# Expert selection placed one head earlier among the gathers, and up rows taken from the first free group on, in a two-layer transformer kernel on one core

## The chip, the cores and the metric

The kernel runs on one core of one Trainium2 chip. The metric is the device time of one execution in microseconds (us), lower is better. The engines named below are PE (TensorE, matrix products), DVE (VectorE), ACT (ScalarE), POOL (GpSimd, here the issuer of the gathers), and SP (SyncE, issuer of plain loads). All loads and gathers share the core's 16 DMA engines.

## The reference, cut to what matters

Two layers over 256 tokens of width 2048. The first is attention plus a state-space branch, followed by a retrieval block of single-neuron experts; the second has dilated attention and latent attention. The change lies in the retrieval block:

```
q = (ht @ w_query).reshape(t_, PEER_HEADS, 2, PEER_HALF)          # 8 heads, 2 halves
v1, i1 = lax.top_k(s1, 16); v2, i2 = lax.top_k(s2, 16)            # scores against 128 keys each
cand = (v1[..., :, None] + v2[..., None, :])                      # 256 candidates
top_s, pos = lax.top_k(cand, 16); idx = take_along_axis(...)      # 16 experts of 16384
gate = jax.nn.softmax(top_s, axis=-1)
u_sel = expert_down[idx]; act = einsum('tkd,td->tk', u_sel, hb)   # 128 down rows per token
w = gate * gelu(act)
return einsum('tk,tkd->td', w, expert_up[idx])                    # 128 up rows per token
```

## The kernel before, in words

The 256 tokens are two tiles of 128, and 8 retrieval heads for each tile make 16 "heads" here, 0 to 15. The order is 0 and 1 (tile 0), 2 and 3 (tile 1), and so on, so that four heads share one round of keys. Each head has 16 experts per token. **Row k.n** is the n-th down row of head k for all 128 tokens: one gather of 128 x 2048 floats, 1.05 MB. **Dot k.n** is the DVE instruction that multiplies row k.n with the tokens and sums (L2229).

**POOL** issues the gathers in order of k.n (`load_down`, L2219), each by the expert numbers of its head. There are 8 places for down rows (`DOWN_BUFS`), so row k.n may be issued only when the dot 8 rows earlier has ended. Before row 0 of heads 2, 4, 8 and 12, POOL also waits for `experts_ready`, the expert numbers that DVE selects. Among the gathers stand "early" up rows (`load_up`, L2270, 128 x 1280 floats, 0.66 MB, the left five eighths of an up row): one after each of rows 3.5 to 3.15, 7.5 to 7.15, 11.6 to 11.15, and one after each row of heads 14 and 15. This order isn't changed.

**DVE** runs a loop over heads h = 0 to 14 and slots n = 0 to 15; slot (h, n) holds dot (h+1).n, then what `rows_dve` puts there, then for h = 13 and 14 the marking of a group (below). `rows_dve` spreads the selection (`choose`) of later heads over such slots in seven steps: step 0 and 1 take the best 16 of 128 key scores, steps 2 and 3 the best 16 of 256 sums, steps 4 and 5 turn positions into expert numbers (step 5 releases `experts_ready`, L2142), step 6 finishes the gates. Selection number 2 is for heads 2 and 3, number 3 for heads 4 to 7, number 4 for heads 8 to 11, number 5 for heads 12 to 15. ACT takes the exponentials for the gates between steps 3 and 6 (`take_gates`).

**The dense part.** The right three eighths of the up rows aren't gathered. For these the weights are spread into a matrix over all 16384 experts, per tile in 32 groups of 4 tokens (64 groups in all): DVE marks (`mark_group`, 1 + 4 instructions, L2366 and L2371), PE multiplies (`spread_group`, L2381), ACT stores (`take_group`, L2389). Groups 0 to 28 stand in the slots of h = 13 and 14, groups 29 to 63 in a free loop behind the last head. From group 32 on, the second tile's, the weights of that tile must have been turned by PE (`turn_weights(pe, 1)`) and stored by ACT (`take_weights(act, 1)`). Then `dense_rows` (L2411) multiplies with the up rows' right part, which SP loads.

**Up rows in the middle.** Up rows 64 to 95 are handled in 16 pairs in the free loop: of each pair PE sums the first (`sum_up`, L2313), with a diagonal matrix from ACT (`spread_weight`), and DVE adds the second (`add_up`, L2279). They have 5 places. All later up rows, 96 to 255, are added by DVE alone, while the dense products run on PE. `add_sums` (L2323) adds a PSUM sum to the result; `add_sums(dve, 1)` must come before PE begins the next sum.

## Time and profile before

| | us |
|---|---|
| median of 3 runs (3607.11 to 3608.49) | 3607.83 |
| the profiled execution, its own time | 3608.36 |
| its span, first to last instruction | 3606.6 |

| stretch of the span | us | what runs |
|---|---|---|
| 870.85 to 1420.55 | 549.70 | dots of heads 1 to 11 |
| 1420.55 to 1644.20 | 223.65 | dots of heads 12 to 15, groups 0 to 28 |
| 1644.20 to 1740.20 | 96.00 | groups 29 to 63, up rows 64 to 95 |
| 1740.20 to 2137.50 | 397.30 | dense products, up rows 96 to 255 |

The profiled execution's own time is 1.8 us more than its span. The rest of the kernel, before and behind these stretches, holds none of the code that changes. The row stretches begin at the first dot of a head; in a list of dots their starts are the first dot's starts.

### The profile page before, as it was taken

What the parts mean: (1) busy time and instruction counts of PE and PEld (TensorE: products, weight loads), DVE (VectorE), ACT (ScalarE), POOL (GpSimd) and SP (SyncE); (2) the same over time, 40 slices, a digit from 0 to 9 for tenths busy, and PEclk for the clock granted to TensorE, in tenths of its full rate; (3) what the DMA queues carried; (4) which work ended last, traced back from release to release, by engine and by line L of the source; (5) the groups of instructions that cost most, each with busy time, mean ns of one, the idle gap of its engine ahead of it and who ended that gap; (6) DMA issues with size and microseconds to landing.
All of it is one profiled execution on the core that took longest, in us unless ns stands there. A gap on an engine that the chain in (4) does not pass through costs nothing.

```text
span 3606.6 us, 39375 instructions
## 1 busy us (share of the span) xinstructions
PE 2995.7 (83%) x13798; PEld 2309.4 (64%) x13798; DVE 2075.7 (58%) x3044; ACT 1314.6 (36%) x1921; POOL 2328.1 (65%) x1216
## 2 busy tenths in 40 slices
PE   9999999993636303278999829999999999999998
PEld 7888878872312101145555418888888888888887
DVE  8998264239898999888765652221332222425444
ACT  6776575441000000023100004444444444445553
POOL 2021767876768686854433437887787778878665
PEclk9999999997868656699999969999999999999999
DMA  7455545669899999997999975555555555555445
GB/s 230 141 149 143 169 145 165 210 194 388 356 377 417 377 420 371 420 364 260 358 409 409 398 247 169 175 170 170 168 176 175 169 175 170 175 187 173 149 146 169
DMA packets 251357, 886.67 MB, mean 246 GB/s; under 512 B 30240, under 2 KB 33440, under 8 KB 217376
## 3 DMA queue, kind: packets, MB, share of 16 engines
q1 hardware_dynamic: 171424, 442.36, 38.7%
q0 software_dynamic: 76288, 438.08, 30.6%
q10 hardware_dynamic: 3456, 3.77, 0.3%
q8 instruction: 111, 1.82, 0.2%
q14 instruction: 78, 0.64, 0.1%
HBM read 876.77 MB, written 2.10 MB: 244 GB/s over the span
## 4 chain that ended last, share of the span: by engine, by line
PE 60%; DVE 13%; DMA 11%; POOL 10%; issue 3%; DVEq 2%; ACT 1%; ACTq 0%; SPq 0%
PE products L759 41%; DMA arena<-up_left_in,arena 9%; POOL arena L2219 9%; PE products L1630 6%; DVE arena L2229 4%; PE products L2313 2%; DVE arena L2279 2%; DMA arena<-peer_down_in,arena 1%; PE products L2381 1%; PE products L1300 1%; PE products L2969 1%; POOL arena L2270 1%; DVE arena L2371 1%; PE products L1406 1%; PE products L2931 1%
## 5 line engine op out<-in xcount | busy, mean ns | idle before, releaser
L718 POOL TENSOR_TENSOR weights_low<-arena,weights_high 128x1024 fp32r<-128x1024 f32 x484 | 1187.6, 2461 | 386.0 <-ACT weights_high L706 371.9
L759 PE MATMUL products<-weights_high,input_high 128*128 128x512 f32 x2352 | 951.8, 405 | 17.2 <-DVE weights_low L718 15.6
L706 ACT ACTIVATE weights_high<-arena 128x1024 fp32r<-128x1024 f32 x588 | 621.3, 1059 | 902.2 <-PE products L759 842.9
L759 PE MATMUL products<-weights_low,input_high 128*128 128x512 f32 x2352 | 920.7, 391 | 0.0
L759 PE MATMUL products<-weights_high,input_low 128*128 128x512 f32 x2352 | 918.5, 391 | 0.0
L2229 DVE SCALAR_TENSOR_TENSOR arena<-arena 128x2048 f32<-128x2048 f32 x256 | 581.7, 2290 | 57.2 <-DMA arena<-peer_down_in,arena 54.6
L2219 POOL DMA_INDIRECT arena<-peer_down_in,arena x256 | 508.6, 1987 | 154.1 <-issue 73.6
L759 PEld LDWEIGHTS products<-weights_high,input_high 128*128 128x128 f32 x2352 | 443.1, 188 | 106.8 <-DVE weights_low L718 17.3
L759 PEld LDWEIGHTS products<-weights_low,input_high 128*128 128x128 f32 x2352 | 442.2, 188 | 95.6
L759 PEld LDWEIGHTS products<-weights_high,input_low 128*128 128x128 f32 x2352 | 443.4, 189 | 85.9 <-issue 0.2
L2270 POOL DMA_INDIRECT arena<-up_left_in,arena x224 | 259.9, 1160 | 324.2 <-DVE arena L2279 214.3
L2279 DVE SCALAR_TENSOR_TENSOR arena<-arena 128x1280 f32<-128x1280 f32 x176 | 272.6, 1551 | 145.9 <-DMA arena<-up_left_in,arena 144.2
L1565 POOL TENSOR_TENSOR weights_low<-arena,weights_high 128x1024 fp32r<-128x1024 f32 (+2 forms) x115 | 257.2, 2244 | 93.6 <-ACT weights_high L1501 91.6
L2313 PE MATMUL products<-over_halves 128*128 128x512 f32 (+1 forms) x192 | 87.0, 609 | 205.2 <-DMA over_halves<-up_left_in,arena 179.5
L2411 PE MATMUL products<-arena,over_halves 128*128 128x512 f32 (+1 forms) x512 | 190.6, 496 | 14.2 <-DMA arena<-up_right_in 12.5
L2313 PEld LDWEIGHTS products<-over_halves 128*128 128x128 f32 x192 | 40.6, 220 | 250.0 <-issue 222.3
L2411 PE MATMUL products<-arena 128*128 128x512 f32 (+1 forms) x512 | 189.5, 494 | 0.0
L1340 DVE TENSOR_TENSOR arena<-products,arena 128x128 f32<-128x128 f32 x96 | 29.9, 352 | 241.9 <-PE products L1300 241.9
L2442 ACT ACTIVATE arena<-arena 128x16 f32<-128x16 f32 x16 | 3.5, 216 | 449.4 <-DVE arena L2234 449.4
L1501 ACT ACTIVATE weights_high<-arena 128x1024 fp32r<-128x1024 f32 (+2 forms) x112 | 109.0, 974 | 137.7 <-PE products L1630 127.6
L2676 POOL COPY arena<-arena 128x252 f32<-128x252 f32 x16 | 19.8, 1266 | 206.7 <-DVE arena L2771 206.7
L2411 PEld LDWEIGHTS products<-arena,over_halves 128*128 128x128 f32 x512 | 98.2, 194 | 83.2 <-issue 42.4
(394 smaller groups left out, 4200.1 us busy)
## 6 DMA issues: line engine op xcount, KB each, us to landing
arena<-dsa_in SPq DMA_DIRECT2D x320, 512.0 KB, 3.5
arena<-w_in_in SPq DMA_DIRECT2D x128, 512.0 KB, 3.7
arena<-up_right_in SPq DMA_DIRECT2D x128, 384.0 KB, 8.4
arena<-mla_wide_in SPq DMA_DIRECT2D x88, 512.0 KB, 3.5
arena<-w_attn_o_in SPq DMA_DIRECT2D x32, 512.0 KB, 3.8
arena<-w_out_in SPq DMA_DIRECT2D x32, 512.0 KB, 4.7
arena<-peer_w_query_in SPq DMA_DIRECT2D x32, 512.0 KB, 5.0
arena<-dsa_w_out_in SPq DMA_DIRECT2D x32, 512.0 KB, 3.7
```

The costliest lines, as they stand in the source:

```text
L706: nc.scalar.activation(w_hi[:, u % RING, :, at], ring[:, u % RING, :, at], ACT.Copy).then_inc(hi_made, 1)
L718: ops.tensor_tensor(w_lo[:, u % RING, :, at], ring[:, u % RING, :, at], w_hi[:, u % RING, :, at].bitcast(F32), op=ALU.subtract).then_inc(l ...
L759: mm = nc.tensor.matmul(PS[:, bank(b) + t, 0:width], x[:, x0 + n, at], y, start=n == 0 and m == 0, stop=n == len(parts) * PK - 1 and m == 2)
L1501: nc.scalar.activation(mla_half(0, n)[:, at], ringf[:, n % RING, at], ACT.Copy).then_inc(hi_made, 1)
L1565: nc.gpsimd.tensor_tensor(w_lof[:, n % RING, at], ringf[:, n % RING, at], w_hif[:, n % RING, at].bitcast(F32), op=ALU.subtract).then_inc(l ...
L1630: mm = nc.tensor.matmul(banks[:, t, 0:width], x[:, x0 + PK * u + k, q], y, start=u == 0 and k == 0 and m == 0, stop=last and k == PK - 1 a ...
L2219: pool.indirect_dma_start(down_place(j), None, I["peer_down"][0], bass.IndirectOffsetOnAxis(ap=experts[:, r, t, p, n:n + 1], axis=0))\
L2229: nc.vector.scalar_tensor_tensor(out=row, in0=row, scalar=1.0, in1=h2[:, t], op0=ALU.mult, op1=ALU.mult, accum_out=acts[:, h % 2, n:n + 1])\
L2270: pool.indirect_dma_start(up_places[at], None, up_left, bass.IndirectOffsetOnAxis(ap=experts[:, r, t, p, n:n + 1], axis=0))\
L2279: nc.vector.scalar_tensor_tensor(out=X[:, t, 0:LEFT], in0=up, scalar=weights[:, t, h // 4, h % 2, n:n + 1], in1=X[:, t, 0:LEFT], op0=ALU.m ...
L2313: mm = nc.tensor.matmul(PS[:, b, 0:at.stop - at.start], diag_of(m), up[:, at], start=m == first, stop=m == last)
L2411: return nc.tensor.matmul(PS[:, DENSE_BANKS[t, q], 0:at.stop - at.start], spread[t][:, i], dense[place][:, at], start=i == 0, stop=last)
```

## The change

Three edits. Selection 2 runs its steps 0 to 5 in slots 0 to 5 of h = 0 (before: slots 1, 3, ..., 11) and step 6 in slot 13 as before. Selections 3, 4 and 5 move from h = 2, 6, 10 to h = 1, 5, 9, at the same slots; ACT's `take_gates` moves with them. In the free loop the up pairs begin at group 29 rather than at 32: one pair in each of groups 29, 30, 31, then one in every second group up to 57, none in groups 58 to 63 (before: every second group from 33 to 63). For this the turn of the second tile's weights moves behind group 31, and `add_sums(dve, 1)` moves ahead of group 29.

```diff
+def middle_pair(g):
+
+    first = FIRST_FREE_GROUP
+    if g < TILE_GROUPS:
+        return g - first if g >= first else None
+    return TILE_GROUPS - first + (g - TILE_GROUPS) // 2 if g % 2 and g < 2 * TILE_GROUPS - 2 * (TILE_GROUPS - first) else None
...
-            if h in (2, 6, 10) and n == 9:
+            if h in (1, 5, 9) and n == 9:
                 take_gates(act, h // 4 + 3)
...
-            if h == 0 and n % 2 and n // 2 < CHOICES:
-                choose(dve, 2, n // 2)
+            if h == 0 and n < CHOICES - 1:
+                choose(dve, 2, n)
+            if h == 0 and n == TOPK - 3:
+                choose(dve, 2, CHOICES - 1)
...
-            if h in (2, 6, 10) and n % 2 and n // 2 < CHOICES:
+            if h in (1, 5, 9) and n % 2 and n // 2 < CHOICES:
                 choose(dve, h // 4 + 3, n // 2)
...
             dve.drain()
+            add_sums(dve, 1)
             for g in range(FIRST_FREE_GROUP, GROUPS):
                 mark_group(dve, g)
-                if g == TILE_GROUPS - 1:
-                    add_sums(dve, 1)
-                if g >= TILE_GROUPS and g % 2:
-                    add_up(dve, EARLY_UPS + g - TILE_GROUPS)
+                if middle_pair(g) is not None:
+                    add_up(dve, EARLY_UPS + 2 * middle_pair(g) + 1)
...
-            turn_weights(pe, 1)
             for g in range(FIRST_FREE_GROUP, GROUPS):
+                if g == TILE_GROUPS:
+                    turn_weights(pe, 1)
                 spread_group(pe, g)
-                if g >= TILE_GROUPS and g % 2:
-                    sum_up(pe, EARLY_UPS + g - TILE_GROUPS - 1)
+                if middle_pair(g) is not None:
+                    sum_up(pe, EARLY_UPS + 2 * middle_pair(g))
```

ACT's part of the free loop follows PE's in the same way. POOL's and SP's instructions stay as they are, in order and in what they wait for.

**DVE, the first dots of head 2** (places are `down_in` numbers, the row's number modulo 8). Before, dots follow each other:

```order
789 L2229 SCALAR_TENSOR_TENSOR arena<-arena 128x2048 [waits down_in0]
790 L2229 SCALAR_TENSOR_TENSOR arena<-arena 128x2048 [waits lo_made,down_in1]
791 L2229 SCALAR_TENSOR_TENSOR arena<-arena 128x2048 [waits down_in2]
792 L2229 SCALAR_TENSOR_TENSOR arena<-arena 128x2048 [waits down_in3]
793 L2229 SCALAR_TENSOR_TENSOR arena<-arena 128x2048 [waits down_in4]
```

After the change, step 0 of selection 3 stands behind dot 2.1:

```order
789 L2237 SCALAR_TENSOR_TENSOR arena<-arena 128x2048 [waits down_in0]
790 L2237 SCALAR_TENSOR_TENSOR arena<-arena 128x2048 [waits lo_made,down_in1]
791 L2094 MAX arena<-arena 128x8 [waits key_scores_in]
792 L2094 MAX arena<-arena 128x8 x7
793 L2097 MAX_INDEX arena<-arena 128x8
```

The selection's instructions have moved over from the dots of head 3, whose dots now follow each other; heads 6 and 7, and 10 and 11, change in the same way.

**PE, the start of the free loop** behind group 28 (L2342 turns the weights, L2381 is a group, L2313 sums an up row). Before:

```order
3642 L2342 MATMUL products<-arena 128x128 [waits picks_here,weights_ready]
3643 L2381 MATMUL products<-arena 128x128 [waits spread_read,hots_made]
3644 L2381 MATMUL products<-arena 128x128 x3
3645 L2381 MATMUL products<-arena 128x128 [waits spread_read,hots_made]
3646 L2381 MATMUL products<-arena 128x128 x3
3647 L2381 MATMUL products<-arena 128x128 [waits spread_read,hots_made]
```

After (L2350, L2389 and L2321 are the same three lines):

```order
3651 L2321 MATMUL products<-arena 128x256
3652 L2389 MATMUL products<-arena 128x128 [waits spread_read,hots_made]
3653 L2389 MATMUL products<-arena 128x128 x3
3654 L2321 MATMUL products<-arena 128x512 [waits up_in_third4,diag_ready]
3655 L2321 MATMUL products<-arena 128x512
3656 L2321 MATMUL products<-arena 128x256
3657 L2350 MATMUL products<-arena 128x128 [waits picks_here,weights_ready]
```

The turn of the weights now stands behind the third sum, where it was ahead of the first group.

## Rows read from the trace of the kernel before

**Rows 1.** The cores' spans and granted clock.
```profile
core 0: 3606.6 us, clock 0.925
```
**Rows 2.** Windows: us; busy us and instructions of PE, PEld, DVE, ACT, POOL; PEclk; DMA share; GB/s
```profile
870.85:926.95 56.10, 24.94 (x56) 11.35 (x57) 53.69 (x102) 2.82 (x6) 24.19 (x13) 0.68 0.79 309
926.95:974.85 47.90, 32.95 (x77) 14.25 (x75) 36.97 (x35) 0.70 (x3) 42.42 (x19) 0.89 1.02 416
974.85:1041.57 66.72, 34.53 (x94) 18.19 (x94) 63.96 (x152) 9.02 (x21) 39.80 (x26) 0.76 0.92 370
1041.57:1081.50 39.93, 0.00 (x0) 0.00 (x0) 36.68 (x36) 0.34 (x2) 35.06 (x17) 0.50 1.00 408
1081.50:1126.72 45.22, 44.32 (x98) 19.67 (x99) 36.85 (x35) 1.18 (x4) 40.34 (x17) 0.94 1.02 417
1126.72:1167.73 41.01, 13.27 (x31) 5.51 (x29) 36.85 (x35) 0.70 (x3) 35.83 (x18) 0.73 1.01 419
1167.73:1234.45 66.72, 32.60 (x90) 16.86 (x90) 63.95 (x153) 8.91 (x21) 39.99 (x27) 0.76 0.91 369
1234.45:1274.53 40.08, 0.00 (x0) 0.00 (x0) 36.77 (x35) 0.34 (x2) 35.20 (x17) 0.50 1.01 409
1274.53:1314.35 39.82, 0.00 (x0) 0.00 (x0) 36.86 (x35) 1.07 (x3) 34.94 (x17) 0.50 1.01 420
1314.35:1354.18 39.83, 0.00 (x0) 0.00 (x0) 36.86 (x36) 0.35 (x2) 34.96 (x17) 0.50 1.01 420
1354.18:1420.55 66.37, 27.28 (x64) 13.30 (x64) 63.96 (x153) 6.16 (x14) 41.94 (x27) 0.71 0.89 361
...
1644.20:1740.20 96.00, 80.53 (x391) 55.33 (x391) 87.28 (x204) 41.64 (x56) 45.07 (x33) 0.95 0.70 228
```
**Rows 3.** Waits of POOL from 870 to 1650: us in total, times, longest.
```profile
POOL arena L2219 <- DVE arena L2142: 50.1, 4, 15.1
...
POOL arena L2219 <- DVE arena L2229: 19.6, 7, 4.5
```
**Rows 4.** Timeline of POOL in head 7: start, us, instruction, idle before.
```profile
1177.09 0.94 POOL L2270 DMA_INDIRECT over_halves<-up_left_in,arena  x1 [0.30 <-issue]
1178.34 2.99 POOL L2219 DMA_INDIRECT arena<-peer_down_in,arena  x1 [0.31 <-issue]
...
1224.29 2.75 POOL L2219 DMA_INDIRECT arena<-peer_down_in,arena  x1 [12.44 <-DVE arena L2142]
```
**Rows 5.** Timeline of DVE: dots 7.11 to 7.15 and 8.0.
```profile
1217.12 2.29 DVE L2229 SCALAR_TENSOR_TENSOR arena<-arena 128x2048 f32<-128x2048 f32 x1
...
1223.94 2.28 DVE L2229 SCALAR_TENSOR_TENSOR arena<-arena 128x2048 f32<-128x2048 f32 x1
...
1229.38 2.29 DVE L2229 SCALAR_TENSOR_TENSOR arena<-arena 128x2048 f32<-128x2048 f32 x1
...
1231.59 2.29 DVE L2229 SCALAR_TENSOR_TENSOR arena<-arena 128x2048 f32<-128x2048 f32 x1
...
1234.45 2.29 DVE L2229 SCALAR_TENSOR_TENSOR arena<-arena 128x2048 f32<-128x2048 f32 x1
```
**Rows 6.** Windows of 10 us around the end of selection 4, columns as in rows 2.
```profile
1210.00:1220.00 10.00, 9.58 (x28) 5.09 (x27) 9.44 (x14) 2.49 (x4) 0.94 (x1) 0.99 1.01 416
1220.00:1230.00 10.00, 4.43 (x12) 1.82 (x10) 9.39 (x15) 0.00 (x0) 5.10 (x3) 1.00 0.34 110
```
**Rows 7.** Timeline of POOL, the first up row issued after a long pause.
```profile
1665.58 1.87 POOL L2270 DMA_INDIRECT arena<-up_left_in,arena  x1 [20.61 <-PE products L2313]
```
**Rows 8.** Chain that ended last, the same up row: start, us from issue to landing.
```profile
1665.58 5.48 DMA arena<-up_left_in,arena
```
**Rows 9.** Timeline of DVE at the end of the groups.
```profile
1738.58 1.62 DVE L2323 TENSOR_TENSOR arena<-products,arena 128x512 f32<-128x512 f32 x3 [1.94 <-PE products L2313]
1740.29 7.77 DVE L2279 SCALAR_TENSOR_TENSOR arena<-arena 128x1280 f32<-128x1280 f32 x5
1749.22 1.55 DVE L2279 SCALAR_TENSOR_TENSOR arena<-arena 128x1280 f32<-128x1280 f32 x1 [1.17 <-DMA arena<-up_left_in,arena]
1752.72 1.55 DVE L2279 SCALAR_TENSOR_TENSOR arena<-arena 128x1280 f32<-128x1280 f32 x1 [1.95 <-DMA arena<-up_left_in,arena]
```

More of the change, by code:

```diff
@@ L3300, in _ @@
                     take_picks(act)
-                if h in LAST_OF_TILE:
-                    take_weights(act, LAST_OF_TILE.index(h))
+                if h == LAST_OF_TILE[0]:
+                    take_weights(act, 0)
                 for n in range(TOPK):
@@ L3309, in _ @@
             for g in range(FIRST_FREE_GROUP, GROUPS):
-                if g >= TILE_GROUPS and g % 2 == 0:
-                    spread_weight(act, EARLY_UPS + g - TILE_GROUPS)
+                if g == TILE_GROUPS:
+                    take_weights(act, 1)
+                if middle_pair(g) is not None:
+                    spread_weight(act, EARLY_UPS + 2 * middle_pair(g))
                 take_group(act, g)
@@ L3494, in _ @@
                         spread_group(pe, group_of(h, n))
-            turn_weights(pe, 1)
             for g in range(FIRST_FREE_GROUP, GROUPS):
+                if g == TILE_GROUPS:
+                    turn_weights(pe, 1)
                 spread_group(pe, g)
-                if g >= TILE_GROUPS and g % 2:
-                    sum_up(pe, EARLY_UPS + g - TILE_GROUPS - 1)
+                if middle_pair(g) is not None:
+                    sum_up(pe, EARLY_UPS + 2 * middle_pair(g))
             dense_rows(pe)
```

## The prediction, made before the changed kernel was run

> **What bounds the kernel now.** I read the windows by head first, then the waits of POOL, then single rows of POOL and DVE. The reader should see two kinds of head. In heads 8, 9, 10 [rows 2] the DMA share is 1.01 at 409 to 420 GB/s, DVE is busy 36.8 of 39.8 us: DMA is the bound, and 39.82 / 16 = 2.49 us is what one down row costs it. An up row has 5/8 of the bytes, 0.655 MB / 420 GB/s = 1.56 us. In heads 3, 7 and 11 DVE is busy 64.0 of 66.4 to 66.7 us: there the selection lies between the dots and DVE is the bound. The early up rows travel in just these heads: 16 x 2.49 + 11 x 1.56 = 57.0 us of DMA work (one up row less in head 11) under 66.7 us of DVE work. What is left is a hole: POOL has no expert numbers and waits for L2142, four times, 50.1 us in all [rows 3], 12.44 us at the end of selection 4 [rows 4], and the DMA rate falls to 110 GB/s [rows 6]. But the queue still holds rows when POOL stops, so DMA loses less than POOL waits: against 420 GB/s, head 1 (309) loses 14.8 us, head 3 (370) 7.9, head 7 (369) 8.1, head 11 (361) 9.3, in sum 40 us [rows 2]. That is the most that earlier numbers could give back.
>
> **The selection moved: the same steps, other neighbours.** The steps cost DVE the same wherever they stand. A dot follows a dot in 2.21 us (1229.38 to 1231.59), the end of a head adds 0.65 (1231.59 + 2.21 to 1234.45) [rows 5], so a head without selection needs DVE for 16 x 2.21 + 0.65 = 36.0 us, and selections 3 to 5 add 66.7 - 36.0 = 30.7 us; step 5 is 1223.94 - 1217.12 - 2.21 = 4.6 us and step 6 is 1.0 (1229.38 - 1226.15 - 2.21, dot 7.13 starting 2.21 behind 1223.94) [rows 5]. After the change this work lies in heads 2, 6, 10, where only down rows are issued, and the up rows lie in heads 3, 7, 11, which DVE can pass in 36 us but DMA needs 57 us for.
>
> What could save it is reading ahead in the long head: rows come at 2.49 us and are used every 66.7 / 16 = 4.2 us. But there are 8 places. The question is therefore how far DMA has got when the selection ends. I take t = 0 at the end of dot 6.11. Step 5 ends at 4.6, dot 6.12 at 6.8, dot 6.13 at 9.0, step 6 at 10.0, dots 6.14 and 6.15 at 14.4, and dot 7.0 starts at 15.1. Row 7.4 needs the place of 6.12, free at 6.8; POOL's issue takes 2.75 us while dots run [rows 4] and ends at 9.9. From the end of an issue to the landing on an empty queue an up row took 5.48 - 1.87 = 3.6 us [rows 7, 8], a down row so 3.6 - 1.56 + 2.49 = 4.5: row 7.4 lands at 14.4. Row 7.5's issue follows, ends 0.9 us behind dot 6.14 at 13.1, and the row lands at 17.6. From there DMA is never short of work: 10 rows of head 7, row 8.0 and 11 up rows are 11 x 2.49 + 11 x 1.56 = 44.6 us, so dot 8.0 starts at 62.2. **Head 7 then takes 62.2 - 15.1 = 47.1 us**, head 3 the same, head 11 with ten up rows 45.5. The point at which the move pays nothing is easy to give: heads 6 and 7 together take 41.0 + 66.7 now (head 6 a little over 39.8), 66.7 + X then, with X for head 7; X = 39.8 to 41 is even, and 47.1 is 6 to 7 us above it.
>
> The sum over heads 1 to 11, before [rows 2]: 56.1 + 47.9 + 66.7 + 39.9 + 45.2 + 41.0 + 66.7 + 40.1 + 39.8 + 39.8 + 66.4 = 549.7. After: 56.1 + 66.7 + 47.1 + 39.9 + 45.2 + 66.7 + 47.1 + 39.8 + 39.8 + 66.4 + 45.5 = 560.3. So **+10.6 us**. Why each stays: head 1 is filled by DVE (53.7 of 56.1) whichever slot selection 2 has; head 5 carries query weights beside the rows and keeps them. Head 2 carried such weights too (47.9 rather than 39.8); under a selection they are hidden, which is why the first three heads come out nearly even (169.9 against 170.7) although selection 2's 15.1 us wait [rows 3] goes. Heads 12 to 15 start from the same state, DVE waiting for rows, and only shift.
>
> New waits: step 0 of selection 3 now needs its key scores in slot 1 of head h = 1; ACT stores them in slot 9 of h = 0, eight slots earlier, so nothing. Behind a waiting step all dots would queue, and POOL behind these through the places. ACT's `take_gates` moves along with step 3, and what follows it on ACT (the diagonals for the early up rows) comes free earlier; no gain, since DMA bounds those heads.
>
> The waits of POOL [rows 3] alone would promise 50.1 us, a time near 3558; the same hole stands at the end of each of the four selections, and it is the places that bound what replaces it. Perfetto Trace Analysis, section Optimization Strategy, of the Trainium skill says that a bubble which repeats on the engine that should be saturated can mean too few buffers for the next tile. By that rule the bubble only moves to where the 8 places run out, and next to nothing of the 50 us comes back.
>
> **The free loop.** DVE's work from 1644.2 to 1740.2 is 87.3 of 96.0 us [rows 2], and nothing is added or taken. At its end 1.94 us of waiting for PE's last sum [rows 9] goes, since the last pair is now in group 57. A wait of the same kind appears: group 32 needs the turned weights, which now stand behind three sums on PE. I put 1.94 back, net 0, with -2.5 and +3 as ends (no wait; one up row's 3.6 us late as well). The DMA pause of 20.61 us ahead of up row 69 [rows 7] moves to the six last groups, so at the end all five places are full. The five adds take 7.8 us either way, then DVE waits 1.17 and 1.95 us [rows 9] where about 1 us each is the pace of that stretch; with full places both come down to that pace, 1.1 us less. DMA bounds what follows, so this stays: -1.1 us, with 0 and -3.1 (two up rows) as ends.
>
> **Sum.** +10.6 + 0 - 1.1 = +9.5 on the profiled 3608.4 (span 3606.6 [rows 1] and 1.8 around it), 3617.9, which is 0.5 above the median of the runs shown: 3617.4, I say 3617.5.
>
> **Rivals.**
> *Places suffice, faster.* If by the end of the selection enough rows lie ready, heads 3, 7, 11 go at DVE's 36.0 us: 11.1 + 11.1 + 9.5 = 31.7 us less, 3586. For it: in head 1, already under a selection, POOL waits for dots only 19.6 us over the whole stretch [rows 3], and the queue carries it some way. Against: DMA would need 4 to 5 rows more than the places allow. It decides from X below 39.8. Chance 0.08.
> *It cancels.* X near 43, because issues fall into pauses between dots (0.94 us rather than 2.75 [rows 4]) and rows 7.4 and 7.5 land 2 us earlier each: 3 x 4.1 less, 3605. The move that does nothing, a POOL that still waits somewhere else as long as before, is in this case too. Chance 0.30.
> *POOL limits the up rows, slower still.* In heads 3, 7, 11 dots run back to back as long as rows lie ready, and an issue then ends only behind a dot (2.75 and 2.99 us against 0.94 [rows 4]). A pair of row and up row costs POOL 2 x 2.21 = 4.42 us where DMA needs 4.05: up to 11 x 0.37 = 4 us more a head, 12 in all, 3629. Against: once DVE waits for rows, POOL is free of it. Chance 0.14. SBUF — State Buffer, section Who interferes with whom, of the Trainium skill describes this as an exclusive lock on a port pair that DVE and GpSimd share; by that rule POOL would be blocked for a whole dot, as the rows show.
> *The forecast*, X from 44 to 50: 0.48.
>
> **How the numbers follow.** Three like runs spread by 1.4 us; about 0.2%, 7.2 us, can be told from no change. Slower by more means over 3615.0: the forecast (0.48, less 0.02 for its lower edge) and the last rival (0.14), 0.60. Same: 0.32. Faster: 0.08. The range leaves out the faster case and the far end of the slowest: 3603 to 3629.
>
> **What would show it.** POOL's wait for the selection's cast (50.1 us) is gone, and its wait for dots grows from 19.6 to some 60 us. Heads 2, 6, 10 take 66.7 us with DVE busy 64 and a DMA rate near 300 GB/s; heads 3, 7, 11 take 47 us at 420 GB/s with DVE waiting. The groups' stretch stays at 96 us within 3, with its DMA pause at the end. The forecast is wrong if head 7 comes out under 41 us, if a selection step waits for key scores, or if the groups' stretch moves by over 5 us.

## The result, and the profile after

| | us |
|---|---|
| kernel after, median of 4 runs (3637.64 to 3641.59) | 3638.39 |
| kernel before, median of 4 runs beside it (3607.11 to 3608.87) | 3608.16 |
| ratio after to before, 95% interval | 1.0086 [1.0068, 1.0103] |
| span of the profiled execution after | 3635.8 |

The change costs 30 us. The prediction was 3617.5 with a range up to 3629: the side was right, the size a third of what came, and the measured time lies outside the range. The cores' view of the kernel after, to be held against [rows 1]:

```profile
core 0: 3635.8 us, clock 0.924
```

The two profiled spans differ by 29.2 us. Cut at the same events (first dot of heads 1, 12 and 15, end of dot 15.15, end of the groups, landing of the last up row), the difference lies here:

| stretch | before | after | difference | predicted |
|---|---|---|---|---|
| up to dot 1.0 | 870.9 | 871.8 | +1.0 | 0 |
| heads 1 to 11 | 549.7 | 576.6 | **+26.9** | +10.6 |
| heads 12 to 14 | 153.3 | 153.6 | +0.2 | 0 |
| head 15 | 70.3 | 73.5 | +3.2 | 0 |
| groups 29 to 63 | 96.0 | 97.8 | +1.8 | 0 (-2.5 to +3) |
| late up rows | 395.7 | 394.9 | -0.8 | -1.1 |
| the rest | 1470.7 | 1467.6 | -3.1 | 0 |

The windows of the kernel after, heads 1 to 11 and then the groups' stretch, columns as in [rows 2]:

```profile
871.82:927.93 56.11, 33.79 (x73) 15.04 (x74) 53.70 (x102) 2.82 (x6) 26.81 (x16) 0.74 0.89 346
927.93:994.87 66.94, 25.51 (x60) 11.04 (x58) 64.26 (x153) 3.53 (x6) 32.32 (x17) 0.71 0.83 317
994.87:1047.84 52.97, 34.63 (x92) 17.14 (x93) 36.41 (x35) 6.53 (x18) 45.05 (x27) 0.85 1.00 392
1047.84:1088.03 40.19, 0.45 (x5) 0.21 (x2) 36.96 (x35) 0.34 (x2) 35.31 (x17) 0.55 1.01 421
...
1133.28:1199.83 66.55, 12.57 (x30) 5.29 (x28) 64.13 (x153) 3.53 (x6) 33.43 (x18) 0.63 0.80 309
1199.83:1252.01 52.18, 33.64 (x90) 16.73 (x90) 36.50 (x35) 6.41 (x18) 44.56 (x26) 0.85 1.00 390
1252.01:1292.18 40.17, 0.01 (x1) 0.00 (x0) 36.95 (x34) 0.34 (x2) 35.29 (x17) 0.55 1.01 421
...
1332.00:1398.53 66.53, 0.00 (x0) 0.00 (x0) 64.12 (x152) 3.05 (x5) 34.36 (x19) 0.50 0.80 305
1398.53:1448.44 49.91, 28.15 (x62) 12.79 (x63) 36.34 (x36) 3.67 (x11) 42.59 (x25) 0.82 1.00 395
...
1675.53:1773.32 97.79, 81.16 (x391) 54.96 (x391) 87.20 (x204) 40.66 (x56) 44.68 (x33) 0.95 0.72 238
```

Heads 2, 6 and 10 are as drawn: 66.5 to 66.9 us with DVE busy 64 of them and the DMA rate at 305 to 317 GB/s. Heads 3, 7 and 11 are DVE's 36.4 us of work in 53.0, 52.2 and 49.9 us, at 390 to 395 GB/s where the neighbours reach 421. The prediction said 47.1, 47.1 and 45.5. These three terms are 15.4 us of the 20 that are missing in the sum.

POOL's waits of the kernel after, from 870 to 1680, against [rows 3]:

```profile
POOL arena L2227 <- DVE arena L2237: 116.7, 25, 6.6
...
POOL arena L2278 <- PE products L2321: 45.5, 26, 4.4
```

The 50.1 us of waiting for the selection's numbers are gone from the list, and its wait for dots, which means for places, has grown from 19.6 to 116.7 us, twice the 60 that I had foretold. POOL waits more than before.

The chain that ended last, head 7 of the kernel after (start, us, what):

```profile
1191.87 2.76 POOL arena L2227
1194.93 2.94 POOL arena L2227
1198.17 1.90 POOL over_halves L2278
...
1200.38 2.55 POOL arena L2227
...
1203.24 1.91 POOL over_halves L2278
1205.45 1.91 POOL arena L2227
...
1218.82 0.94 POOL arena L2227
1220.07 2.50 POOL over_halves L2278
```

Row 7.4 is issued at 1191.87, behind dot 6.12, and dot 7.0 starts at 1199.83, 15 us after dot 6.11 ends: the places do what the prediction said. But the chain then runs through POOL, issue by issue. At first one issue ends per dot, 2.21 us apart (1203.24 to 1205.45), 4.42 us for a row and its up row; later a pair is 0.94 + 2.50 and two gaps of 0.30, from start to start 4.06 us, just DMA's own 4.05. DVE meets this from dot 7.7 on (its timeline; before that the dots follow each other):

```profile
1215.41 2.29 DVE L2237 SCALAR_TENSOR_TENSOR arena<-arena 128x2048 f32<-128x2048 f32 x1
...
1219.47 2.29 DVE L2237 SCALAR_TENSOR_TENSOR arena<-arena 128x2048 f32<-128x2048 f32 x1 [1.76 <-DMA arena<-peer_down_in,arena]
...
1223.54 2.29 DVE L2237 SCALAR_TENSOR_TENSOR arena<-arena 128x2048 f32<-128x2048 f32 x1 [1.77 <-DMA arena<-peer_down_in,arena]
```

Dots 7.7 to 8.0 are nine steps in 1252.01 - 1215.41 = 36.6 us, 4.07 each, the full rate. So the head loses its 5 us ahead of row 7.7. That row landed 15.6 us after dot 7.0 began; at full rate (2.5 us to row 7.5, then two pairs of 4.05) it would have been 10.6. The two windows show it, 333 GB/s and then 415:

```profile
1199.83:1215.39 15.56, 7.88 (x17) 4.10 (x18) 15.56 (x15) 3.79 (x11) 13.43 (x8) 0.61 0.95 333
1215.39:1252.01 36.62, 25.76 (x74) 12.63 (x72) 20.94 (x21) 2.62 (x7) 31.14 (x19) 0.95 1.01 415
```

Of this, POOL's spacing would explain a part: its issues of rows 7.5 and 7.7 end at 1197.87 and 1207.36, 9.5 us apart for 8.1 us of DMA work, 1.4 us. The other 3.2 us lie between issue and landing: row 7.5 landed 4.8 us behind the end of its issue (1202.70), row 7.7 8.0 us behind (1215.39).

**Head 15**, whose instructions didn't change, took 3.2 us more. Windows of 5 us, and PE's timeline in them:

```profile
1607.00:1612.00 5.00, 3.69 (x6) 1.52 (x5) 5.00 (x10) 1.22 (x2) 1.95 (x1) 0.58 0.94 349
1612.00:1617.00 5.00, 3.68 (x13) 2.78 (x12) 5.00 (x11) 1.23 (x2) 3.32 (x2) 0.73 0.29 110
```
```profile
1602.19 2.42 PE L2321 MATMUL products<-arena 128*128 128x512 f32 x6 [1.39 <-ACT arena L2305]
...
1608.47 4.63 PE L2321 MATMUL products<-arena 128*128 128x512 f32 x6 [1.31 <-ACT arena L2305]
```

PE's granted clock fell for some us to its lower level, 1.2 GHz (0.58 on the mean of the window), although PE had been busy 3.3 to 3.7 of every 5 us before, and one up row's sum took 4.63 rather than 2.42 us. POOL's next up row waited for its place 4.43 us instead of some 2.3, the row gathers queued behind it, and DMA ran dry (110 GB/s). Of the 15 profiles of this study four show such a fall at this place, between 5 and 15 us after dot 15.0 starts (granted clock of the first 5 us of it 0.58 to 0.70): this one, e3, e6 and e8. Their head 15 took 73.5, 74.0, 71.8 and 73.2 us; in the eleven others, with 1.00 throughout the head, it took 69.7 to 71.4. Selections 3 to 5 and the loop of e3 are those of before, so the 3 us are an event that comes and goes, and not the change's; why the clock fell is not shown.

**The free loop.** DVE's timeline of the kernel after, at its start and at its end, against [rows 9]:

```profile
1695.20 1.55 DVE L2287 SCALAR_TENSOR_TENSOR arena<-arena 128x1280 f32<-128x1280 f32 x1 [4.46 <-DMA arena<-up_left_in,arena]
1696.94 0.69 DVE L2374 TENSOR_TENSOR arena<-arena 128x512 f32<-128x512 f32 x1 [0.19 <-ACT arena L2362]
...
1771.70 1.61 DVE L2331 TENSOR_TENSOR arena<-products,arena 128x512 f32<-128x512 f32 x3
1773.41 7.76 DVE L2287 SCALAR_TENSOR_TENSOR arena<-arena 128x1280 f32<-128x1280 f32 x5
1782.24 1.58 DVE L2287 SCALAR_TENSOR_TENSOR arena<-arena 128x1280 f32<-128x1280 f32 x1 [1.07 <-DMA arena<-up_left_in,arena]
1785.20 1.55 DVE L2287 SCALAR_TENSOR_TENSOR arena<-arena 128x1280 f32<-128x1280 f32 x1 [1.38 <-DMA arena<-up_left_in,arena]
```

The wait for the turned weights, which I had put at 1.94 us, is 0.19. The wait for up row 69 is real and is 4.46 us: it needs the place of row 64, whose sum now is the first thing in the loop. At the end PE's 1.94 us are gone and the adds behind the five wait 1.07 and 1.38 rather than 1.17 and 1.95. Net +1.8 and -0.8.

These two differences are from one profile each, and the others of the study set them in proportion. With the loop of before (six profiles) the groups' stretch takes 94.5 to 97.0 us, mean 95.6; with the new loop (nine) 96.0 to 99.6, mean 98.0: the edit costs about 2.4 us there. The late up rows take 394.9 us on the mean of the six and 395.7 on that of the nine: no gain can be seen. The last stretch takes 1467.3 to 1470.7 us in all profiles but one (e5, 1475.6), so the kernel before is the longest of the rest and the -3.1 us of the table is scatter.

### The profile page after: what moved, and what is told of

It reads as the page before. It is cut to its first block, busy times and chain, and to the rows that moved or that the text cites. A ratio compares the mean times of both kernels' runs of the same rounds, so it can differ in the third digit from the quotient of the medians.

```text
span 3635.8 us, 39375 instructions
## 1 busy us (share of the span) xinstructions
PE 3000.1 (83%) x13798; PEld 2310.2 (64%) x13798; DVE 2076.0 (57%) x3044; ACT 1315.5 (36%) x1921; POOL 2332.1 (64%) x1216
## 3 DMA queue, kind: packets, MB, share of 16 engines
q0 software_dynamic: 76288, 438.08, 30.7%
## 4 chain that ended last, share of the span: by engine, by line
PE 67%; DVE 12%; POOL 10%; DMA 5%; issue 3%; DVEq 2%; ACT 1%; ACTq 0%; SPq 0%; POOLq 0%
PE products L767 41%; PE products L2419 7%; POOL arena L2227 7%; PE products L1638 6%; DVE arena L2237 4%; DMA arena<-up_left_in,arena 3%; PE products L2321 2%; POOL over_halves L2278 2%; DMA arena<-peer_down_in,arena 1%; PE products L2389 1%; DVE arena L2287 1%; PE products L1308 1%; PE products L2979 1%; DVE arena L2379 1%; PE products L1414 1%
## 5 line engine op out<-in xcount | busy, mean ns | idle before, releaser
L767 PE MATMUL products<-weights_high,input_high 128*128 128x512 f32 x2352 | 952.9, 405 | 15.4 <-DVE weights_low L726 13.8
L2227 POOL DMA_INDIRECT arena<-peer_down_in,arena x256 | 489.0, 1910 | 196.9 <-DVE arena L2237 123.9
L1573 POOL TENSOR_TENSOR weights_low<-arena,weights_high 128x1024 fp32r<-128x1024 f32 (+2 forms) x115 | 257.7, 2250 | 91.8 <-ACT weights_high L1509 89.8
L2321 PE MATMUL products<-over_halves 128*128 128x512 f32 (+1 forms) x192 | 90.0, 614 | 203.0 <-DMA over_halves<-up_left_in,arena 203.0
L2321 PEld LDWEIGHTS products<-over_halves 128*128 128x128 f32 x192 | 39.6, 220 | 252.1 <-issue 244.1
L2419 PE MATMUL products<-arena 128*128 128x512 f32 (+1 forms) x512 | 186.7, 488 | 0.0
L790 PE MATMUL products<-arena 128*128 128x128 f32 x176 | 28.6, 289 | 177.9 <-ACT arena L2600 98.9
L1509 ACT ACTIVATE weights_high<-arena 128x1024 fp32r<-128x1024 f32 (+2 forms) x112 | 109.0, 975 | 137.2 <-PE products L1638 127.4
L2321 PE MATMUL products<-arena 128*128 128x512 f32 (+1 forms) x288 | 120.7, 557 | 41.6 <-ACT arena L2305 38.1
```

Source lines behind the costliest of these rows:

```text
L767: mm = nc.tensor.matmul(PS[:, bank(b) + t, 0:width], x[:, x0 + n, at], y, start=n == 0 and m == 0, stop=n == len(parts) * PK - 1 and m == 2)
L1509: nc.scalar.activation(mla_half(0, n)[:, at], ringf[:, n % RING, at], ACT.Copy).then_inc(hi_made, 1)
L1573: nc.gpsimd.tensor_tensor(w_lof[:, n % RING, at], ringf[:, n % RING, at], w_hif[:, n % RING, at].bitcast(F32), op=ALU.subtract).then_inc(l ...
L2227: pool.indirect_dma_start(down_place(j), None, I["peer_down"][0], bass.IndirectOffsetOnAxis(ap=experts[:, r, t, p, n:n + 1], axis=0))\
L2321: mm = nc.tensor.matmul(PS[:, b, 0:at.stop - at.start], diag_of(m), up[:, at], start=m == first, stop=m == last)
L2419: return nc.tensor.matmul(PS[:, DENSE_BANKS[t, q], 0:at.stop - at.start], spread[t][:, i], dense[place][:, at], start=i == 0, stop=last)
```

## The experiments

Thirteen kernels. Times are medians; a ratio is to the kernel before beside it, with its 95% interval. The heads' times are from one profile each, between the starts of their first dots in the list of dots. After and e1 have the same code here, and their heads 3, 7, 11 differ by up to 1.1 us: so much is scatter.

| kernel | 1 | 2 | 3 | 6 | 7 | 10 | 11 | 1 to 11 | time |
|---|---|---|---|---|---|---|---|---|---|
| before | 56.1 | 47.9 | 66.7 | 41.0 | 66.7 | 39.8 | 66.4 | 549.7 | 3608.16 |
| after | 56.1 | 66.9 | 53.0 | 66.5 | 52.2 | 66.5 | 49.9 | 576.6 | 3638.39 |
| e1 selections only | 56.1 | 66.9 | 52.0 | 66.5 | 52.5 | 66.5 | 51.0 | 577.0 | 3638.97 |
| e2 loop only | 56.1 | 47.9 | 66.7 | 41.0 | 66.7 | 39.8 | 66.4 | 550.6 | 3612.13 |
| e3 selection 2 only | 56.1 | 42.8 | 66.7 | 41.0 | 66.7 | 39.8 | 66.4 | 544.5 | 3603.15 |
| e4 up rows too | 56.1 | 66.8 | 36.0 | 66.5 | 36.0 | 66.4 | 36.0 | 526.3 | 3582.55 |
| e5 half way | 56.1 | 54.1 | 54.9 | 51.7 | 54.9 | 50.4 | 55.0 | 531.1 | 3590.54 |
| e6 narrow up rows | 56.1 | 66.9 | 50.9 | 66.6 | 51.9 | 66.5 | 49.8 | 578.4 | 3635.43 |
| e7 up rows too, old loop | 56.1 | 66.8 | 36.0 | 66.5 | 36.0 | 66.4 | 36.0 | 526.4 | 3577.69 |
| e8 up rows alone | 56.1 | 63.8 | 67.3 | 62.6 | 67.0 | 57.0 | 66.7 | 603.1 | 3657.38 |
| e9 half dots | 56.1 | 66.9 | 51.3 | 66.6 | 52.4 | 66.8 | 49.4 | 575.4 | 3637.04 |
| e10 half dots, narrow | 56.1 | 66.9 | 42.6 | 66.5 | 44.3 | 66.8 | 42.6 | 552.9 | 3614.66 (one run) |
| e11 after, 7 places | 56.1 | 66.9 | 54.8 | 66.5 | 54.4 | 66.5 | 53.6 | 584.5 | 3647.88 |
| e12 before, 7 places | 56.3 | 48.4 | 66.9 | 41.0 | 66.9 | 39.9 | 66.5 | 551.0 | 3611.36 |
| e13 later up rows | 56.1 | 66.9 | 47.5 | 66.5 | 46.3 | 66.5 | 44.0 | 569.9 | 3634.23 |

**e1, e2, e3: the change taken apart.** e1 is the diff without its free loop, e2 the free loop alone, e3 the edit of selection 2 alone.

> Selections 2 to 5 placed as in the change, the free loop as before. Theory (the selection does nearly all of it): heads 1 to 11 take 576 to 577 us as after the change, the groups' stretch about 96, and head 15 again about 3 us more than before; time 3636 to 3638. Rival (a third of the 30 us comes from the free loop): 3625 to 3630.

Measured 3638.97 us, 1.0079 [1.0064, 1.0095]; heads 1 to 11 take 577.0 us. The selections do nearly all of it. The 3 us in head 15, which I had expected again, weren't there (70.5), so they don't come from the selection.

> Only the free loop as in the change, selections as before. Theory: heads 1 to 11 take 549.7 us again, the groups' stretch 1.8 us more (the up row that POOL issues late now stops DVE near the start of the loop), the dense stretch 0.8 us less: time 3607 to 3611, the same within 0.2%. Rival (the free loop causes a third of the loss): 3615 or more. Second rival (the 3 us that head 15 grew came from the loop's order): head 15 takes over 73 us here.

Measured 3612.13 us, 1.0009 [1.0000, 1.0018]: 2.4 us more by the medians, 3 by the ratio with 0 and 6.5 as ends, so the same within 0.2% and no third of the loss. Head 15 took 70.5 us, so the loop's order doesn't lengthen it. In its profile the groups' stretch is 3.4 us longer and the one behind it 1.4 shorter.

> Only selection 2 in slots 0 to 5 of head 1, all else as before. Theory: POOL's wait of 15.1 us for selection 2 goes, but head 1 is filled by DVE (53.7 of 56.1 us) and so keeps its 56 us; head 2 may start with more rows ready and come out a little under 47.9. Time 3605 to 3609. Rival (expert numbers come too late, and this wait is real time): 3598 or less. Rival (earlier steps starve the queue the other way): 3612 or more.

Measured 3603.15 us, 0.9979 [0.9970, 0.9988], 6.6 us less by the medians: more than I gave it, less than the rival. Its windows, heads 1 and 2:

```profile
870.91:927.01 56.10, 33.77 (x75) 15.05 (x76) 53.69 (x102) 2.81 (x6) 26.79 (x16) 0.75 0.88 345
927.01:969.81 42.80, 25.05 (x59) 10.83 (x57) 36.54 (x36) 0.74 (x3) 37.93 (x17) 0.86 1.02 416
```

Head 1 keeps its 56.1 us, as DVE fills it, but DMA moves 345 GB/s in it instead of 309 [rows 2], and these 2 MB or two rows are the 5.1 us that head 2 needs less. In the kernel after, the same gain is lost, because head 2 is then bound by DVE and has no use for rows that lie ready.

**e4 and e8: which neighbour matters.** e4 moves the early up rows with the selection, e8 moves them without it:

```diff
-UP_SLOTS = [(h, n) for h, first in ((2, 5), (6, 5), (10, 6)) for n in range(first, TOPK)] + \
+UP_SLOTS = [(h, n) for h, first in ((1, 5), (5, 5), (9, 6)) for n in range(first, TOPK)] + \
```

> The changed kernel with its early up rows moved one head earlier as well (after rows 2.5 to 2.15, 6.5 to 6.15, 10.6 to 10.15), so that they lie beside the selection again; as many gathers, only their neighbours differ. Theory (the loss is that the up rows have lost the selection as cover): heads 2, 6, 10 take 66.7 us with the up rows in them, heads 3, 7, 11 fall from 50 to 53 to about 40; against the change 12 x 3 = 36 us less, against the kernel before about 8 less, since the query weights of head 2 are then hidden too: about 3600. Rival (the loss is in the selection's early place itself, through places and the restart of the queue, whatever travels beside it): heads 3, 7, 11 stay above 45 and the time above 3620.

Measured 3582.55 us, 0.9919 [0.9904, 0.9934], 56 us less than the kernel after with as many gathers. Heads 3, 7 and 11 fell to 36.0 us, DVE's own pace, and not to 40: with the up rows beside the selection DMA doesn't stop, and the next head starts with its places full. The direction was foretold, the size was 18 us short.

> The kernel before with its early up rows alone moved one head earlier; the selections stay. The selection is again separated from the up rows, the other way round. Theory (separation is what costs, in either direction): heads 2, 6, 10 become DMA bound with 57 us of work (65 with head 2's weights), heads 3, 7, 11 stay at the selection's 66.4 to 66.7 us: heads 1 to 11 take 590 to 600 us, time 3645 to 3660. Rival (what costs is the selection's early place, through the places and POOL's restart, not the separation): the time stays within 5 us of before.

Measured 3657.38 us, 1.0128 [1.0111, 1.0144], heads 1 to 11 603.1 us, 3 beyond the range that I gave. Separated in the other direction the same two things cost 49 us by the medians (46 by the ratio). Both kernels together settle the main question: it is not the early place that costs, it is the up rows' loss of their cover.

The cover has two halves. One is time, DVE's 30.7 us of selection. The other is POOL's. In the kernel before, 217 of the 218 issues that began 0.1 us or more into a dot ended 0.8 us behind it, and took up to 3.0 us; of the 39 that began so in a one-input step of a selection (MAX8, FIND_INDEX8, MATCH_REPLACE8 and its load), 38 took 0.94. In head 7 of the kernel before, with DVE in such a step:

```profile
1185.09 0.94 POOL L2270 DMA_INDIRECT over_halves<-up_left_in,arena  x1 [0.30 <-issue]
1186.34 0.94 POOL L2219 DMA_INDIRECT arena<-peer_down_in,arena  x1 [0.30 <-issue]
```

Beside a selection POOL so gets ahead: row 7.13 of the kernel before landed 16.8 us behind the end of its issue, row 7.7 of the kernel after 8.0.

**e7: the best version.** As e4, with the free loop of the kernel before.

> Selections and early up rows both one head earlier, as in e4_ups_too, the free loop as before. Theory (the free loop's edit costs about 2 us, as the run of the loop alone says): 3578 to 3582, 1 to 4 us under e4_ups_too. Rival (the loop's edit gains once the rows are early, since DMA is the bound behind it): 3584 to 3588.

Measured 3577.69 us, 0.9909 [0.9893, 0.9926], 30.6 us under the kernel before beside it (3608.31) and faster than every other kernel of this study. Against e4 (3582.55) it is 4.9 us less by the medians; the two ratios' intervals overlap, so this agrees with e2's 3 us for the loop's edit and doesn't size it better. Its windows, heads 6, 7 and 8:

```profile
1113.50:1180.00 66.50, 52.80 (x127) 25.43 (x128) 64.09 (x152) 6.85 (x16) 43.70 (x28) 0.86 1.02 418
1180.00:1216.00 36.00, 18.16 (x60) 9.21 (x59) 35.59 (x35) 2.70 (x7) 31.12 (x17) 0.84 1.02 420
1216.00:1254.80 38.80, 0.00 (x0) 0.00 (x0) 36.52 (x35) 0.34 (x2) 33.65 (x17) 0.50 1.01 421
```

DVE is busy 64.1 of 66.5 and 35.6 of 36.0 us while DMA moves 418 to 420 GB/s: for once both limits are met together, where the kernel before reached 369 GB/s in head 7 and the kernel after 309 in head 6.

**e5: half way.** Selections 3 to 5 start four slots earlier than before instead of sixteen, on the kernel after:

```diff
-            if h in (1, 5, 9) and n % 2 and n // 2 < CHOICES:
-                choose(dve, h // 4 + 3, n // 2)
+            k = TOPK * h + n - 29
+            if 0 <= k < 3 * 4 * TOPK and k % (4 * TOPK) % 2 == 0 and k % (4 * TOPK) // 2 < CHOICES:
+                choose(dve, k // (4 * TOPK) + 3, k % (4 * TOPK) // 2)
```

> The changed kernel, but selections 3 to 5 begin only 4 slots earlier than before (step 0 behind dots 2.13, 6.13, 10.13) instead of 16, so that step 5 ends behind dot 3.7 and row 4.0 finds its numbers in time, while most of the up rows behind rows 3.5 to 3.15 still travel beside the selection. Theory (a selection must cover its up rows, and only then is lead worth something): POOL's wait for the numbers gone and heads 2 and 3 together 103 to 109 us against 114.6 before and 119.9 after the change: time 3585 to 3600. Rival (any earlier place than that of before lets the places run out and costs time, in proportion to the shift): 3612 to 3620.

Measured 3590.54 us, 0.9937 [0.9918, 0.9956]. Heads 2 and 3 take 109.0 us against 114.6 and 119.9, and head 4 another 3.9 less. So, with the up rows left where they are, lead is worth something when it is just enough for row 4.0, and turns into a loss when it grows to sixteen slots: the rival's proportion is refuted.

**e6, e9, e10: what makes heads 3, 7, 11 longer than 47.1 us.** e6 gathers the 32 early up rows as 128 x 128, e9 cuts each dot of these heads in two, e10 does both. e6 sums the gathered tenth of an up row ten times over and e9 leaves the second half's sum out of the dot, so all three compute something else than the reference:

```diff
+            if m < EARLY_UPS // 2:
+                pool.indirect_dma_start(up_places[at][:, 0:128], None, up_left.rearrange("r (a c) -> (r a) c", a=10),
...
-            nc.vector.scalar_tensor_tensor(out=row, in0=row, scalar=1.0, in1=h2[:, t],
...
+            halves = [slice(0, D // 2), slice(D // 2, D)] if h in (3, 7, 11) else [slice(0, D)]
+            for half in halves:
```

> The changed kernel, its 32 early up rows gathered a tenth as wide (128 x 128 instead of 128 x 1280; the sums read these columns ten times over, so the output is another): POOL issues as many gathers, DMA moves 0.06 MB in place of 0.66 MB. DMA work of heads 3, 7, 11 falls from 44.6 to about 30 us, below DVE's 36.0. Theory A (the 5 us by which these heads exceeded 47.1 are DMA's, rows landing slowly behind an empty queue): heads 3, 7, 11 take 36 to 38 us. Theory B (they are POOL's, one issue per running dot, 2.21 us each, 4.42 a pair, against 2.29 of work on DVE): POOL needs 11 pairs, 48.6 us, less what it is ahead, so the heads take 44 us or more and dots wait for rows that POOL has not issued.

Measured 3635.43 us, and heads of 50.9, 51.9 and 49.8 us: theory B. DMA had its work cut to two thirds and ran at 0.74, and nearly nothing came back. The window of head 7, and a part of its chain:

```profile
1200.38:1252.30 51.92, 35.99 (x90) 17.78 (x90) 36.39 (x35) 6.43 (x18) 44.61 (x25) 0.83 0.74 257
```
```profile
1210.44 1.90 POOL arena L2227
...
1212.64 1.92 POOL over_halves L2279
...
1214.87 1.90 POOL arena L2227
...
1217.07 1.92 POOL over_halves L2279
```

A row follows a row in 1214.87 - 1210.44 = 4.43 us, which is two dots (2 x 2.21). That holds as long as dots follow each other, to 1220. From row 7.9 on DVE waits for each row and runs one dot a pair, and the pace is still the same, for another reason:

```profile
1225.99 2.91 POOL over_halves L2279
1229.20 0.94 POOL arena L2227
```

A dot starts as its row lands (1225.78), the up row's issue begins just behind it and is held for the whole dot (2.91 us), then comes the row's (0.94): with two gaps of 0.30 that makes 4.45 us, and POOL is idle for no longer than such a gap. Rows 7.7 to 8.0 took 39.9 us for nine steps, 4.43 each, against 4.07 in the kernel after. The relief of DMA brought row 7.7 earlier (9.3 us behind row 7.5 instead of 12.7, no more than its issue is behind row 7.5's), and POOL's pace gave it back.

> The changed kernel, but in heads 3, 7, 11 each dot is two instructions of 128 x 1024 (the second half's sum is thrown away, so the output is another). DVE does the same work in pieces of about 1.1 us, so POOL's issue, which ends 0.9 us behind the running piece, takes at most about 2 us instead of up to 2.9. Theory (POOL is the limit of these heads because its issues wait for the dots): a row and its up row cost POOL under 4.05 us, DMA becomes the limit and heads 3, 7, 11 take 46 to 49 us; time 3622 to 3628. Rival (POOL's issue is slow for another reason, or rows land slowly behind an empty queue): they stay at 50 to 53 us and the time at 3636 to 3641.

Measured 3637.04 us, 1.0070 [1.0052, 1.0088], heads of 51.3, 52.4 and 49.4: the rival's numbers came, the theory's didn't. Windows of head 7 of e9 and of e10, and POOL's timeline of e9 in it:

```profile
1198.32:1250.71 52.39, 37.40 (x90) 17.84 (x90) 37.60 (x68) 6.42 (x18) 38.79 (x29) 0.78 1.00 393
```
```profile
1191.24:1235.54 44.30, 33.42 (x90) 16.70 (x90) 37.44 (x67) 6.42 (x18) 36.68 (x26) 0.87 0.84 305
```
```profile
1202.96 1.99 POOL L2227 DMA_INDIRECT arena<-peer_down_in,arena  x1 [0.30 <-issue]
1205.25 1.98 POOL L2281 DMA_INDIRECT over_halves<-up_left_in,arena  x1 [0.30 <-issue]
1207.54 1.99 POOL L2227 DMA_INDIRECT arena<-peer_down_in,arena  x1 [0.31 <-issue]
```

The edit doesn't do at first what I wanted of it: an issue ends 0.8 us behind a half dot, the next begins 0.3 later and so falls into the half after the next, and POOL goes at 2.29 us an issue as long as halves follow each other. Only from row 7.10 on, where dots wait for rows, do its issues fall to 0.94 to 1.8 us and POOL runs ahead (row 8.0 lands 14.8 us behind the end of its issue); and there DMA is at full share and lets a pair through in 4.07 us.

> The last two together: half dots in heads 3, 7, 11 and early up rows a tenth as wide. Theory (POOL first, DMA second): with both relieved the heads fall further, to 37 to 44 us, below what either alone gives. Rival (something else holds them): 47 or more.

Measured 3614.66 us in one run; the heads take 42.6, 44.3 and 42.6 us. Narrow rows alone gave back 2.5 us over the three heads, half dots alone 2.0 (neither much above scatter), both together 25.6. So heads 3, 7 and 11 stand under two limits that lie 0.36 us a pair apart, POOL's 4.43 and DMA's 4.07, and whoever lifts one meets the other.

**e11 and e12: the places.** Both kernels with 7 places:

```diff
-DOWN_BUFS = 2 * ROWS
+DOWN_BUFS = 2 * ROWS - 1
...
-            return (up_rows if j % DOWN_BUFS < ROWS else down_rows)[:, j % ROWS]
+            p = (j + 3) % DOWN_BUFS
+            return (up_rows if p < ROWS else down_rows)[:, p % ROWS]
```

> The changed kernel with 7 places for down rows instead of 8. Theory (the places bound how far the gathers get under the selection): row 7.4 may be issued only behind dot 6.13, which ended 2.2 us after dot 6.12; so heads 3, 7 and 11 each grow by 2.2 to 2.5 us, to about 55.4, 54.6 and 52.3, while heads 2, 6, 10 stay at 66.5 to 66.9; heads 1 to 11 take 583 to 585, the time 3644 to 3648. Rival (the places don't matter, it is the early place of the selection or the restart alone): heads 3, 7, 11 as in the changed kernel within 1 us, time 3636 to 3641.

Measured 3647.88 us, 1.0102 [1.0086, 1.0119]; heads 1 to 11 take 584.5 us, 7.9 more than with 8 places, nearly all in heads 3, 7, 11 (1.8, 2.2 and 3.7).

> The kernel before with 7 places for down rows instead of 8. Theory (there the hole is set by the expert numbers, which come behind dot 3.11, not by the places, and the up rows fill the queue under the selection): heads 3, 7, 11 stay at 66.4 to 66.7 us, heads 1 to 11 take 550 to 553 us, time 3608 to 3612. Rival (every restart of the queue costs by the places, here too): heads 1 to 11 grow by the same 7 us or more, time 3615 or more.

Measured 3611.36 us, 1.0002 [0.9992, 1.0011]; heads 1 to 11 take 551.0 us. A place is worth 2 to 4 us a selection after the change and nothing that these runs can tell before it. The places bound the gathers after the change only.

**e13: the up rows three rows later**, the last question: does POOL's doubled work or the queue's restart cost the 5 us ahead of row 7.7? On the kernel after:

```diff
-UP_SLOTS = [(h, n) for h, first in ((2, 5), (6, 5), (10, 6)) for n in range(first, TOPK)] + \
+UP_SLOTS = [(h + n // TOPK, n % TOPK) for h, first in ((2, 8), (6, 8), (10, 9)) for n in range(first, TOPK + 3)] + \
```

> The changed kernel with the same 32 early up rows three rows later each: behind rows 3.8 to 4.2, 7.8 to 8.2, 11.9 to 12.2, so that only down rows are issued while the queue starts again. Heads 3 and 4 of the changed kernel take 93.2 us together, 7 and 8 92.4, 11 and 12 91.8; at full rate behind row 7.5 they would be 5 us less each. Theory A (the 5 us are lost because the up rows double POOL's issues just while the dots run back to back): the pairs of heads fall by 3 to 5 us each, time 3624 to 3630. Theory B (rows land slowly behind an empty queue whoever is issued, as rows 4.1 to 4.5 of the kernel before did, 15.0 us for five rows): they fall by at most 2 us each, time 3632 to 3640.

Measured 3634.23 us, 1.0076 [1.0059, 1.0093]. Windows of heads 7 and 8:

```profile
1200.47:1246.80 46.33, 25.11 (x72) 13.15 (x72) 36.16 (x36) 6.20 (x18) 39.62 (x23) 0.80 1.00 394
1246.80:1291.70 44.90, 7.16 (x19) 3.18 (x18) 36.93 (x34) 0.31 (x2) 39.11 (x20) 0.69 1.01 421
```

Together 91.2 us (heads 3 and 4 take 92.4, 11 and 12 90.6) against 92.4 (93.2, 91.8): 0.8 to 1.2 us less each, theory B. That is about the 1.4 us which POOL's spacing was worked out to cost, and about as much as the heads' scatter. Nor does the edit free POOL wholly: the pairs from row 7.8 on still meet dots that follow each other, and go at 4.42 us. So it shows that most of the 5 us isn't due to the up rows standing where they do, and no more than agrees with the 1.4.

## Why the prediction was wrong

**The bound and the hole**: right. DMA lost 40 us in the four selections, and a version that uses them (e7) is 30.6 us faster.

**The same steps, other neighbours**: right, and shown by e4 and e8. Heads 2, 6, 10 were to take 66.7 and took 66.9, 66.5, 66.5.

**The places**: right, and shown by e11 and e12. Row 7.4 was to land 0.7 us before dot 7.0 and landed at 1199.17, 0.7 before 1199.83; row 7.5 was to come 2.5 us after that dot's start and came at 2.9. The rule of the Trainium skill that I cited (Perfetto Trace Analysis, section Optimization Strategy: repeated bubbles can mean too few buffers) agrees for the kernel after. For the kernel before it would have misled: with one buffer less its time is the same.

**"From there DMA is never short of work"**: this step failed. It priced the 11 rows, 44.6 us, at the rate of a queue that is full. The queue had just run empty, and its first rows landed at 333 GB/s: rows 7.5 to 7.7 took 12.7 us for 8.1 us of work. That makes heads 3, 7, 11 5.9, 5.1 and 4.4 us longer than predicted, 15.4 together. Row 7.5 to row 8.0 took 49.3 us where the sum had 44.6. Of the 5.1 in head 7, 0.4 are row 7.5's, 1.4 by this reckoning POOL's spacing of issues by the dots, and 3.2 the time from issue to landing, which grew from 4.8 to 8.0 us in three rows. e6 and e13 agree with this split and don't prove it (with narrow up rows the 3.2 are gone); what in the queue causes them isn't shown. The warning stood in the trace of before, unread: there too, the stretch behind the hole was not at 2.49 us a row. Rows 4.1 to 4.5 had all landed 15.0 us behind row 4.0, where 12.5 were due.

**POOL limits the up rows**, the last rival with 0.14: its mechanism is real, 4.42 us a pair forecast and 4.43 measured in e6, and POOL is what the chain runs through in the kernel after. It isn't the whole of the excess: of head 7's 5.1 us it explains 1.4, and where POOL was freed (e9, behind row 7.10) DMA was the limit at once. What I held against it, that POOL is free once DVE waits for rows, is refuted by e6: there DVE waited about 2 us for every row and POOL still went at 4.43 us a pair. Its 3629 was the nearest of the four numbers. The port rule of the Trainium skill (SBUF — State Buffer, Who interferes with whom) agrees in that an issue ends only behind a running dot. A remark in the same section, marked there as inferred, says that tensor_tensor takes only the shared pair's read interface while descriptor generation needs the write one. It can't be carried over to this DVE instruction, which has two SBUF inputs as well: behind it the issue of a gather took 1.9 to 3.0 us instead of 0.94. Which of the two interfaces the issue waits for isn't shown.

**The other terms.** The free loop was put at 0 with -2.5 to +3 and came to +1.8, about 2.4 over all profiles: the end "one up row late as well" is what happened (4.46 us for row 69, of which the 1.94 at the other end and shorter waits come off); the turned weights cost 0.19 and not 1.94. The tail was -1.1 and measured -0.8, but over all profiles no gain is left, so this hit was luck. Head 15's 3.2 us and the last stretch's -3.1 us cancel, were not in the sum, and come in code that the change doesn't touch; the first goes with a fall of the clock and the second is scatter. Taken together, 15.4 of the missing 19.7 us lie in heads 3, 7 and 11, 1.8 the free loop, 0.3 the tail, 2.2 all that isn't the change's or is spread over other heads.

**Selection 2**: I had written that heads 1 to 3 come out nearly even since head 1 keeps its length. That is so for the three edits together, but e3 shows what it hid: earlier numbers alone are worth 5.1 us in head 2, and moving selection 3 into head 2 throws them away.

## What to carry to other kernels

When work on one engine covers transfers of another, move the two together. Moving either alone cost 30 and 49 us here, moving both gained 30.6. Count, before moving long work ahead, how many buffers' worth of transfers fit under it. And price what comes behind an empty queue by a stretch of the trace that also stands behind one, not by the steady rate. When one relief gives next to nothing, as in e6 and e9, try both before calling the suspect innocent.

## What the runs showed of the hardware

- The same gathers, behind an empty queue, moved 333 GB/s over 15.6 us while the DMA engines were 0.95 busy, and 415 to 421 GB/s from then on. A busy share near 1 doesn't say that the rate is full.
- POOL's issue of a gather ends 0.8 us behind the dot that runs when it starts (217 of 218 in the kernel before); in a selection's MAX8, FIND_INDEX8 and MATCH_REPLACE8 it takes 0.94 us (38 of 39). With dots of 2.21 us back to back that makes one issue per dot; cutting dots in halves made it one per two halves, 2.29 us, no faster.
- PE's granted clock fell to 1.2 GHz for a few us in the midst of matmuls in 4 of 15 profiles, at the same place, and head 15 took 71.8 to 74.0 us in these against 69.7 to 71.4 in the others.
